# One kernel for two chained blocks: an even mixer's low-rank gate in fewer products, finer hand-overs at the norms, and an opening with wide parameter rows

## The reference

```python
# first block, each layer l (DEPTH = 2); mod = silu(c) @ ada_w[l] + ada_b[l], split in nine
n1 = modulate(rms_norm(h, norm_g[l, 0]), sh1, sc1)          # x * (1 + scale) + shift
h = h + 0.5 * g1[:, None, :] * swiglu(n1, ffn_wg[l, 0], ffn_wu[l, 0], ffn_wd[l, 0])
n2 = modulate(rms_norm(h, norm_g[l, 1]), sh2, sc2)
h = h + g2[:, None, :] * token_mixing(n2, ...)               # two attentions, gated
n3 = modulate(rms_norm(h, norm_g[l, 2]), sh3, sc3)
h = h + 0.5 * g3[:, None, :] * swiglu(n3, ffn_wg[l, 1], ffn_wu[l, 1], ffn_wd[l, 1])
# second block, even layer: run once for the context (256 rows) and once for x
qa, ka, va, ga, qb, kb, vb, gb, lr = split_cols(h @ w_in, EVEN_SPLITS)   # lr: 32 columns
lr_f, lr_b = jnp.split(lr, 2, axis=-1)                                   # 16 and 16
def gate(u, w, b):                                                       # w: 16 x 256
    z = (u @ w + b).astype(f32)
    return split_heads(jax.nn.log_sigmoid(z) / GLA_GATE_TAU, GLA_HEADS)
```

## Time and profile before

| what | value |
| --- | --- |
| time, median of 3 runs | 2388.06 (2386.38 to 2388.19) |
| the profiled execution's own time | 2389.25 |
| span of its instructions | 2387.5 |
| PE busy | 2279.4 (95%) |
| DVE busy | 1685.6 (71%) |
| ACT busy | 1049.1 (44%) |
| POOL busy | 108.8 (5%) |
| transfers | 504.16 MB, mean 211 GB/s |
| chain that ended last | PE 84%, DVE 10%, ACT 3%, DMA 2% |
| mean granted clock of TensorE | 0.99 |

### The profile page before, as it was taken

How to read it: one execution, slowest core, us unless ns; L and a number is a source line. 1 busy time by engine, 2 the same in 40 slices (tenths; PEclk the granted TensorE clock), 3 DMA queues, 4 the chain that set the end, 5 groups by cost and what they waited for, 6 DMA issues and landing times.

```text
span 2387.5 us, 43172 instructions
## 1 busy us (share of the span) xinstructions
PE 2279.4 (95%) x18047; PEld 2151.2 (90%) x18070; DVE 1685.6 (71%) x1916; ACT 1049.1 (44%) x1251; POOL 108.8 (5%) x156
## 2 busy tenths in 40 slices
PE   3999999999999999999999999989999999999998
PEld 2999998999999999889998878879998999768997
DVE  4877886787787787678775565778778545686554
ACT  2433556443343345644334434434444444484443
POOL 1000000000000000000000000000000000000000
PEclk8999999999999999999999999999999999999999
DMA  8888764498878867448885324627884554303551
GB/s 285 289 308 297 259 211 143 148 328 306 285 270 303 308 240 242 135 142 318 302 304 162 124 74 142 229 68 267 297 300 160 177 182 158 118 11 132 178 186 59
DMA packets 308649, 504.16 MB, mean 211 GB/s; under 512 B 13042, under 2 KB 240829, under 8 KB 308544
## 3 DMA queue, kind: packets, MB, share of 16 engines
q1 hardware_dynamic: 263392, 340.30, 43.0%
q0 software_dynamic: 41344, 159.39, 18.2%
q10 hardware_dynamic: 3808, 2.97, 0.4%
HBM read 501.58 MB, written 1.05 MB: 211 GB/s over the span
## 4 chain that ended last, share of the span: by engine, by line
PE 84%; DVE 10%; ACT 3%; DMA 2%; issue 2%; ACTq 0%; POOL 0%; DVEq 0%; POOLq 0%
PE banks L517 24%; PE banks L519 24%; PE banks L518 24%; DVE wlo L1618 2%; DMA modw<-in_ada_w_dram 1%; PE banks L679 1%; PE banks L655 1%; PE banks L642 1%; PE banks L541 1%; PE banks L664 1%; DVE arena L1634 1%; ACT whi L1170 1%; PE banks L887 1%; DVE xlo L1795 1%; DVE ecol L2239 0%
## 5 line engine op out<-in xcount | busy, mean ns | idle before, releaser
L517 PE MATMUL banks<-xhi,whi 128*128 128x256 f32 x3616 | 1035.3, 286 | 20.0 <-DVE xlo L1795 13.4
L518 PE MATMUL banks<-xlo,whi 128*128 128x256 f32 x3616 | 1024.5, 283 | 0.0
L519 PE MATMUL banks<-xhi,wlo 128*128 128x256 f32 x3616 | 1024.3, 283 | 0.0
L1618 DVE TENSOR_TENSOR wlo<-stage,whi 128x2048 fp32r<-128x2048 f32 x322 | 736.3, 2289 | 287.4 <-ACT whi L1170 286.2
L1170 ACT CAST whi<-stage 128x2048 fp32r<-128x2048 f32 x322 | 613.5, 1906 | 620.5 <-PE banks L519 589.2
L517 PEld LDWEIGHTS banks<-xhi,whi 128*128 128x128 f32 x3616 | 694.9, 192 | 34.7 <-issue 24.6
L518 PEld LDWEIGHTS banks<-xlo,whi 128*128 128x128 f32 x3616 | 695.2, 192 | 1.1 <-issue 0.5
L519 PEld LDWEIGHTS banks<-xhi,wlo 128*128 128x128 f32 x3616 | 695.2, 192 | 0.0
L517 PE MATMUL banks<-hhi,whi 128*128 128x256 f32 x1536 | 438.1, 285 | 0.3 <-DVE wlo L1618 0.3
L519 PE MATMUL banks<-hhi,wlo 128*128 128x256 f32 x1536 | 434.5, 283 | 0.0
L518 PE MATMUL banks<-hlo,whi 128*128 128x256 f32 x1536 | 434.4, 283 | 0.0
(11 more groups left out here) (246 smaller groups left out, 1704.1 us busy)
## 6 DMA issues: line engine op xcount, KB each, us to landing
stage<-in_mlp_w_dram SPq DMA_DIRECT2D x96, 1024.0 KB, 5.3
modw<-in_w_mod_dram POOLq DMA_DIRECT2D x80, 1024.0 KB, 5.9
modw<-in_ada_w_dram POOLq DMA_DIRECT2D x72, 1024.0 KB, 5.9
stage<-in_ffn_wg_dram SPq DMA_DIRECT2D x44, 1024.0 KB, 5.4
stage<-in_ffn_wu_dram SPq DMA_DIRECT2D x44, 1024.0 KB, 5.4
stage<-in_ffn_wd_dram SPq DMA_DIRECT2D x44, 1024.0 KB, 7.0
stage<-in_ev_w_in_dram SPq DMA_DIRECT2D x24, 1024.0 KB, 5.7
stage<-in_w_in_dram SPq DMA_DIRECT2D x18, 1024.0 KB, 5.5
```

What stands on the lines that cost most here:

```text
L517: mm(out, hi, xh, start=first_mm, stop=False, skip_group_check=True)
L518: mm(out, hi, xl, start=False, stop=False, skip_group_check=True)
L519: return mm(out, lo, xh, start=False, stop=last_mm, skip_group_check=True)
L1618: v.tensor_tensor(wlo[:, s, :], stage[:, s, :], whi[:, s, :].bitcast(F32), ALU.subtract).then_inc(lo_done, 1)
```

## The change

- **Parameters.** The vectors are loaded as wide rows of 1024 (49 rows in 7 transfers) and four narrow ones, the three vectors of scalars are copied to all partitions by the transfer itself, and TensorE turns them block by block; the order within `pcol` is made up by a copy. The wait of SP for a cleared `arena` is gone. `c` comes as rows and is turned by TensorE. `ctx` is loaded later, by POOL, and turned in the joint `n1`.
- **Start vectors.** Scale is made before shift. Quarters 0 to 7 have places of their own (`quarter`): the two `modw` buffers, three in `arena`, `nraw`, the third slot of `stage`; the eighth takes the second `modw` buffer again. POOL waits for all parameters ahead of quarter 3. The last two steps, the second turn and the bias of the shift stand behind the scalings of the norm (`start_shift`). The small scalar operations (`scalars`) stand at the end of `F0`.
- **Weights.** The second chunk of `F0` no longer waits for step 14, the third does.
- **Joints.** `PAIRED` (`n1` to `n5`): VectorE adds the squares of blocks 2, 3 to those of 0, 1, and TensorE sums two blocks where it summed four. `FINE` (the same and `lx2`): blocks 6 and 7 are signalled singly, and the refinement has one operation beside the exponential and three behind it. `SINGLE`: block 0 of the next input is signalled alone. Blank products of `n1`: 14 for 22.
- **Even mixers.** `lrw` has 48 columns (16 forward; 32 forward and backward), so one product of eight gives the forward rows on partitions 0 to 15 and the backward rows on 32 to 47; the bias is the 17th row of the gate's weights, met by a row of ones (`lr_ones`).

```diff
+        def add_wide(name, ap, r):
+            nonlocal nwide
+            row_at[name] = 8 * nwide
+            wide_rows.append((nwide, r, ap))
+            nwide += r
...
+        add_wide("norm_g", A["norm_g"].rearrange("l i d -> (l i) d"), 6)
+        add_wide("b_gate", A["b_gate"].rearrange("l (a d) -> (l a) d", d=D), 4)
+        add_wide("final_g", A["final_g"].rearrange("(a d) -> a d", d=D), 1)
+        add_wide("ada_b", A["ada_b"].rearrange("l (a d) -> (l a) d", d=D), 18)
...
-            "start": ([ada(0, 0), ada(0, 1)], []),
+            "start": ([ada(0, 1), ada(0, 0)], []),
...
+        start_room = {c: arena[:, 4096 + 2048 * (c - 2):4096 + 2048 * (c - 1)] for c in (2, 3, 4)}
+        start_room.update({5: nraw[:].rearrange("p b t -> p (b t)"), 6: stage[:, 2, :]})
+        quarter = lambda c: start_room.get(c, modw[:, c % 2, :])
...
+        PAIRED = ("n1", "n2", "n3", "n4", "n5")
+        SINGLE = ("F0", ("in", 0), "F1", "F2", ("in", 1), "F3", "odx", "M1")
+        FINE = ("n1", "n2", "n3", "n4", "n5", "lx2")
+        early = hid[:, 1, 1, :]
...
+            for o, r, src in wide_rows:
+                sp.dma_start(wide_room[o:o + r, :], src).then_inc(param_landed, 16)
...
+            for at, n, src in ((0, 16, A["od_sink_2"].rearrange("a h -> (a h)")), (16, 8, A["ev_ret_theta_2"].rearrange("a b c -> (a b c)")),
+                               (24, 512, A["lam_p"].rearrange("a b c -> (a b c)"))):
+                sp.dma_start(small[:, at:at + n], src.partition_broadcast(P)).then_inc(param_landed, 16)
...
                 load(n, cols(g, 0))
+                load(n + 1, cols(u, 0))
                 if name == "F0":
                     sp.wait_ge(mod_step, 14)
-                load(n + 1, cols(u, 0))
...
+                low = A["ev_w_in_2"][0].rearrange("(k p) n -> p k n", p=P)
+                sp.dma_start(e["lrw"][:, :, 0:16], low[:, :, 3072:3088]).then_inc(key.sem, key.dma((which, 0)))
+                sp.dma_start(e["lrw"][:, :, 16:48], low[:, :, 3072:3104]).then_inc(key.sem, key.dma((which, 1)))
+                for d in range(2):
+                    sp.dma_start(e["gkw"][32 * d:32 * d + 16, :], A["ev_gla_gk_w_2"][0, d]).then_inc(key.sem, key.dma((which, 2 + 2 * d)))
+                    sp.dma_start(e["gkw"][32 * d + 16:32 * d + 17, :], A["ev_gla_gk_b_2"][0, d:d + 1, :]) \
+                        .then_inc(key.sem, key.dma((which, 3 + 2 * d)))
...
-                    if c >= 2:
-
-                        pool.wait_ge(mod_step, 2 * (c - 1) + 8 * i)
                     src = w[l].rearrange("(k p) n -> p k n", p=P)[:, 2 * q:2 * q + 2, bass.ds(v * 1024, 1024)]
+                    if c < 8:
+
+                        if c == 3:
+                            pool.wait_ge(param_landed, nparam)
+                        if c == 7:
+                            pool.wait_ge(mod_step, 4)
+                        pool.dma_start(quarter(c).rearrange("p (a b) -> p a b", a=2), src).then_inc(start_landed[c], 16)
+                        continue
+
+                    pool.wait_ge(mod_step, 2 * (c - 1) + 8 * i)
                     pool.dma_start(modw[:, c % 2, :].rearrange("p (a b) -> p a b", a=2), src).then_inc(mod_landed[c % 2], 16)
...
+                    if key in PAIRED and h == 0:
+                        pe.wait_ge(dve_out.sem, dve_out.at((key, "pair")))
+                        for k in range(2):
+                            mm(out, ones, src[:, k, :], start=k == 0, stop=False, skip_group_check=True)
+                    if key in PAIRED and h < 2:
+                        continue
+                    if key in FINE and h == 3:
+                        pe.wait_ge(act_out.sem, act_out.at((key, "sq", 6)))
+                        mm(out, ones, src[:, 6, :], start=False, stop=False, skip_group_check=True)
                     pe.wait_ge(act_out.sem, act_out.at((key, "sq", h)))
-                    for k in range(2 * h, 2 * h + 2):
+                    for k in range(7 if key in FINE and h == 3 else 2 * h, 2 * h + 2):
                         last = mm(out, ones, src[:, k, :], start=k == 0, stop=k == 7, skip_group_check=True)
...
+            pe.wait_ge(ident_landed, 16)
+            pe.wait_ge(c_landed, 48)
+            transpose(R[:, 2, 0:3 * KB], crow, 24).then_inc(pe_out.sem, pe_out.next("c"))
...
+            turn_rows(0)
+            rms_stat("n0")
+            pe.wait_ge(act_out.sem, act_out.at("cact"))
+            turn_mod("start", 0)
+            pe.wait_ge(mod_step, 14)
+            pe.wait_ge(act_out.sem, act_out.at(("turned", 0)))
+            keep_warm(Y[:, 0, :], 10)
             turn_mod("start", 1)
-            pe.wait_ge(dve_out.sem, dve_out.at("lam"))
-            mm(R[:, 1, 0:2], ones[0:1, :], stat[0:1, 4:6], start=True, stop=True).then_inc(pe_out.sem, pe_out.next("lam"))
-            pe.wait_ge(act_out.sem, act_out.at(("turned", 1)))
-            keep_warm(Y[:, 0, :], 24)
+            keep_warm(Y[:, 0, :], 12)
...
-                        pe.wait_ge(lrw_landed.sem, lrw_landed.at((which, 2)))
-                        for d in range(2):
-                            for k in range(8):
-                                last = mm(R[0:16, 3, d * T:(d + 1) * T], e["lrw"][:, k, 16 * d:16 * d + 16], nraw[:, k, :],
-                                          start=k == 0, stop=k == 7, skip_group_check=True)
+                        pe.wait_ge(lrw_landed.sem, lrw_landed.at((which, 5)))
+                        for k in range(8):
+                            last = mm(R[0:48, 3, 0:T], e["lrw"][:, k, 0:48], nraw[:, k, :],
+                                      start=k == 0, stop=k == 7, skip_group_check=True)
...
-                        for d in range(2):
-                            for t in range(2):
-                                mm(Y[:, d, t * T:(t + 1) * T], E["lr"][:, d, t * P:(t + 1) * P], e["gkw"][:, d, :],
-                                   start=t == 0, stop=False, skip_group_check=True)
-                                last = mm(Y[:, d, t * T:(t + 1) * T], ones[0:1, :], e["gkb"][:, d, :],
-                                          start=False, stop=True, skip_group_check=True)
+                        for t in range(2):
+                            for d in range(2):
+                                last = mm(Y[:, d, t * T:(t + 1) * T], E["lr"][32 * d:32 * d + 17, t * P:(t + 1) * P],
+                                          e["gkw"][32 * d:32 * d + 17, :], start=t == 0, stop=True, skip_group_check=True)
...
+                    elif key in FINE and h == 3:
+                        act.wait_ge(dve_out.sem, dve_out.at(ready(6)))
+                        done(f(stats_of(key)[0][:, 6, :], src[:, 6, :], ACT.Square), (key, "sq", 6))
+                        act.wait_ge(dve_out.sem, dve_out.at(ready(3)))
+                        done(f(stats_of(key)[0][:, 7, :], src[:, 7, :], ACT.Square), (key, "sq", 3))
+                        continue
...
+                if name == "F0":
+                    scalars()
...
+                if b == 2 and key in PAIRED:
+                    dve.wait_ge(act_out.sem, act_out.at((key, "sq", 1)))
+                    sq = stats_of(key)[0]
+                    done(v.tensor_tensor(sq[:, 0:2, :], sq[:, 0:2, :], sq[:, 2:4, :], ALU.add), (key, "pair"))
...
+                    dve.wait_ge(act_out.sem, act_out.at((key, "ln")))
+                    link(v.tensor_scalar(early, sums, D * eps, -0.5 / D, ALU.add, ALU.mult))
+                    dve.wait_ge(act_out.sem, act_out.at((key, "rstd")))
+                    link(v.tensor_tensor(room, y, y, ALU.mult))
+                    link(v.tensor_tensor(room, room, early, ALU.mult))
+                    link(v.scalar_tensor_tensor(out=y, in0=room, scalar=1.5, in1=y, op0=ALU.add, op1=ALU.mult))
...
+            def start_shift():
+                conv(0)
+                mod_single("start", 1, 6, 8)
+                take_mod(1)
+                mod_bias("start", 1, 2)
+                done(v.memset(stat[:, 61:62], 0.0), "start_shift")
...
+                done(normal(0), (target, "n", "first"))
+                done(normal(1), (target, "n", 0))
+                if late is not None:
+                    for q in range(1, 4):
+                        normal(2 * q)
+                        done(normal(2 * q + 1), (target, "n", q))
+                    late()
+                dve.wait_ge(act_out.sem, act_out.at((target, "xhi", "first")))
+                lo(0).then_inc(x_split.sem, x_split.next((target, "first")))
+                if late is None:
+                    normal(2)
+                    done(normal(3), (target, "n", 1))
+                dve.wait_ge(act_out.sem, act_out.at((target, "xhi", 0)))
+                lo(1).then_inc(x_split.sem, x_split.next((target, 0)))
+                for q in range(1, 4):
+                    if q < 3 and late is None:
+                        normal(2 * q + 2)
+                        done(normal(2 * q + 3), (target, "n", q + 1))
```

(19 more changed lines are left out.)

252 lines of the change are left out of this document (123 added, 129 removed).

## The result

The changed kernel takes 2369.49 (median of four, 2368.09 to 2370.89) against 2387.22 for the kernel before: a ratio of 0.9926, 95% interval 0.9908 to 0.9943. The profiled execution took 2368.84, with a span of 2366.9. So the span is 20.6 shorter, where I had worked out 27.2: faster by 0.7%, inside the range near its slow end, outside the 2356 to 2366 that I had given the forecast itself, and weaker than the sum. It comes nearest to the first rival in time (2369), for other reasons.

The account below looks back on a forecast made before the run. TensorE was taken to bound the kernel outside the opening and joints. Opening -11, joints -1.4 and gate -14.8 sum to -27.2 against 2389.25, giving 2362.0, so a median of 2361; range 2353 to 2370.

Parts of the forecast that it names:

- the first rival: Opening: quarters four to eight wait for parameters landing at 24.2, so the opening gives only 3.5; 2369, chance 0.13.
- The gate: Low-rank gate in both even mixers: fewer, shorter TensorE products and half the clock loss avoided, -14.8.
- Low-rank product: Even mixers: eight products with 48 output rows replace 16 of 16 rows, 3.5 instead of 7.08; -7.0 for both.
- Gate product: Even mixers: four products at 0.35 each, 1.4, replace eight taking 3.66 and 5.10; -6.0 for both.
- Clock: Behind the gate products: the clock's fall, costing 3.6 together, may stay away; half taken, -1.8, bounds 0 and -3.6.
- The opening: Start to second weight chunk: transfers without gaps, first weight product at 53.5, second chunk at 59.3 instead of 70.45; -11.
- The joints: Joints between layers: n1 +0.8, n3 and n4 +0.1 each, n2 and n5 -1.2 each; -1.4 in all.
- the addition that pairs comes a chunk earlier, hidden: At n2 and n5: VectorE's pairing addition, 0.69, costs nothing, leaving -1.2 at each.
- the late parameter gate: Opening: transfers from the fourth quarter on held until parameters land at 24.2, ending at 44.5; 2369, chance 0.13.
- Joints in full: Split not binding n1, n3, n4, and fine first block saving 0.7 in eight places; 2351, chance 0.08.
- a weaker gate: Even mixers: four products don't overlap and the clock falls as before, -10.6 instead of -14.8; 2365, chance 0.12.
- slower: Opening: one queue serves transfers one after another, last quarter lands at 75, first product at 90; 2398, chance 0.03.

## Why the prediction was right, and where it was weak

**The gate (-14.8, measured -16.6)** is right by mechanism and part by part. Low-rank product: -3.42 and -3.43, forecast -7.0 together, measured -6.85. Gate product: -2.58 and -4.03, forecast -6.0, measured -6.6, since four took 1.13 and not 1.4. The row of the attention scores was too dear a neighbour. The Trainium skill's figure (TensorE: Matmul & The Clock Gate, Part 3, "Measured speedup vs the span model") led to an estimate of 0.9 and was as far off on the other side. With what the Trainium skill says there, that small products in different row groups run at once, the trace agrees: the instructions start in pairs, a pair every 0.22, in either order. Clock: I took half of 3.6, and the low clock went at both gates; the steps behind them are -1.48 and -1.67, 3.15 together, so the 3.6 was 0.4 too much. None of the 13 traces with the new gate has low clock at either place, the one trace of before has it at both; that the small products are the cause is likely but not shown, since other places come and go between executions. Half was a guess between none and all.

**The opening (-11, measured -9.2 at the second chunk, where I had forecast it, and -9.8 by the end of `F0`)**, in other executions of the same code up to -11.1 by the end of `F0`. The sum was near for partly wrong reasons. The sixth quarter's steps begin at 30.99, forecast 31.5. I had no wait for TensorE in the chain behind them: the sums of `n0`, 6.71, stand ahead of the first turn on its queue. That is the step that failed: reduction and bias end at 37.0 and not at 35.6, and moving the turn was worth 1.7 to 2.9. Both ends of the chain came 1.8 late by it and by the clock: the first block was there for TensorE near 54.3 and not at 52.5, and the twelve blanks, 0.36 each where 0.21 is the 2.4 GHz level, let the first product in at 55.27 and not at 53.5. That is the time which I had worked out for the rule of the Trainium skill (TensorE: Matmul & The Clock Gate, Part 4) that transposes don't count as activity. The slow blanks right behind the turn agree with it but don't prove it, as TensorE had stood idle for 6.35 before the turn, and that 54.00 came in another execution shows that it isn't all. The gap that the late parameter wait leaves in the transfers is real, and hidden.

**The joints (-1.4, measured +0.7).** `n1`, `n3` and `n4` are right to 0.1, and so is the single block at 0. `n2` and `n5` failed in the step "the addition that pairs comes a chunk earlier, hidden". Its 0.69 is hidden. Its wait for ScalarE isn't: it ends at 444.36, and split and last residual, 2.29 and 0.87, are queued behind it. I had asked what is queued behind the addition at `n1` and not at `n2`, where ScalarE's squares come late because a weight conversion and a table load stand ahead of them. The run with the addition moved gave the forecast gain, 1.17 and 1.18, so the size was right and the place wrong.

**The odd layer (0, measured +4.7)** was no step of mine. I had costed the clock only where the change touches it. The kernel before had lost 8.5 to low clock, the changed one 10.2, in other places; a range of a few multiples of 1.7 on either side belonged into the bounds of every sum here. The median lies 0.5 inside the upper end of the range, less than one such place, so that it fell inside is partly luck. The 6.6 missing from the sum are 1.2 opening, 2.1 joints, 0.4 before `gate1`, 4.7 odd layer, less 1.8 that the gate gave more.

The rivals: the late parameter gate (2369) hit the time and not the cause, and its own test by removal gave nothing. Its sum also has a slip: 7.3 MB at 384 GB/s behind 24.2 end at 43.3 and not at 44.5, which makes it about 2367. Joints in full, a weaker gate and slower are out. The lower end of the range, 2353, follows from none of the sums: the forecast with the bound of the opening gives 2356.

## What to carry to other kernels

When an operation with a wait is put earlier on an engine, cost the wait, not the operation: list what is queued behind it and when what it waits for is really there; moving it behind the next long independent operation gave 1.1 at each of two joints here. When two edits lie on the same chain, each can be worth nothing until the other is done: removing the parameter wait gave nothing that could be told from 0 alone, and 2.2 once the turn was ahead of the sums. And before believing a whole-kernel difference of some microseconds, lay the traces side by side product by product: 4.7 of the 6.6 that seemed missing were lost at places where nothing had been edited.

## What the runs showed of the hardware

- The granted clock falls to its 1.2 GHz level mostly behind idle gaps of TensorE of 1.6 to 2.8, each time for a loss of 1.7 by the clock, or two or three times that in a row. In time one costs 1.5 to 1.7 among weight products and less in an attention. Whether a given gap is followed by it differs between executions of the same code (low at 1800 in one, 1.00 in the other). With blank products in most gaps one trace lost 0, where the same kernel without them lost 11.9; another, with the same blanks, lost 6.8, all of it behind gaps left open.
- Four products of 17 rows and 256 columns, two of them on partitions 0 to 16 and two on 32 to 48, take 1.13 (eight instructions) whether the text alternates between the partitions or not: the instructions start two at a time, a pair every 0.22. Products of 16 rows or one row, all from partition 0 on, started one at a time, 0.23 apart, and so did products of 128 rows with 48 columns of output (16 in 3.65). So few rows alone don't make a product shorter.
